# Two-block transformer stack on one core: feed-forward products of 512 columns on x and its rest side by side

## What is computed

```
def swiglu(h, w_in, w_out):                      # w_in 1024 x 5632, w_out 2816 x 1024
    gate, up = jnp.split(h @ w_in, 2, axis=-1)
    return (jax.nn.silu(gate) * up) @ w_out
...
for l in range(DEPTH):                           # first block
    x = x + 0.5 * swiglu(rmsnorm(x, ffn1_norm[l]), ffn1_w_in[l], ffn1_w_out[l])
    x = x + hybrid_mixer(rmsnorm(x, mix_norm[l]), ...)
    x = x + 0.5 * swiglu(rmsnorm(x, ffn2_norm[l]), ffn2_w_in[l], ffn2_w_out[l])
...
hf = rms_norm(x, g_ffn)                          # second block, end of a layer
x = x + jnp.square(jax.nn.relu(hf @ w_up)) @ w_down
```

## Time and profile before

| what | value |
|---|---|
| median of three runs | 2402.16 us |
| profiled execution, its own time | 2402.9 us |
| its span, first to last instruction | 2401.1 us |
| mean granted TensorE clock | 0.994 |
| TensorE matmul busy | 2356.1 us, 98% |
| weight loads busy | 2219.9 us, 92% |
| VectorE busy | 1588.1 us, 66% |
| ScalarE busy | 1402.8 us, 58% |
| GpSimd busy | 145.8 us, 6% |
| read from HBM | 382.89 MB, 160 GB/s over the span |

### The profile page before, as it was taken

One profiled execution on the slowest core, in us unless ns is written; L12 is line 12 of the kernel. 1 busy time (PEld: TensorE's weight loads), 2 busy tenths in 40 slices (PEclk: granted clock), 3 DMA queues, 4 the chain that ended last, 5 costly groups with the idle time before them and its releaser, 6 DMA issues. The chain is left out here.

```text
span 2401.1 us, 40844 instructions
## 1 busy us (share of the span) xinstructions
PE 2356.1 (98%) x17169; PEld 2219.9 (92%) x17169; DVE 1588.1 (66%) x1951; ACT 1402.8 (58%) x1872; POOL 145.8 (6%) x119
## 2 busy tenths in 40 slices
PE   8999999999999999999999999999999999999998
PEld 7998999999999999899999999899999989999998
DVE  5666668856666656667865656659785554978554
ACT  5455778465555645678835645546854444685443
POOL 0000002200000000001300000000030000004000
PEclk9999999999999999999999999999999999999999
DMA  6554544235555555444424555644555554455653
GB/s 226 194 177 158 158 141 141 89 97 167 193 183 186 177 192 184 151 141 141 127 68 141 173 196 177 199 138 126 157 166 187 195 184 149 124 153 168 206 184 123
DMA packets 312453, 386.57 MB, mean 161 GB/s; under 512 B 10812, under 2 KB 287440, under 8 KB 312272
## 3 DMA queue, kind: packets, MB, share of 16 engines
q1 hardware_dynamic: 311952, 383.86, 49.3%
q10 hardware_dynamic: 320, 0.11, 0.0%
HBM read 382.89 MB, written 1.06 MB: 160 GB/s over the span
## 5 line engine op out<-in xcount | busy, mean ns | idle before, releaser
L313 PE MATMUL bank<-xhi,whi 128*128 128x256 f32 x3712 | 1063.6, 287 | 4.2 <-DVE wlo L302 4.2
L315 PE MATMUL bank<-xhi,wlo 128*128 128x256 f32 x3712 | 1051.2, 283 | 0.0
L314 PE MATMUL bank<-xlo,whi 128*128 128x256 f32 x3712 | 1051.1, 283 | 0.0
L292 DVE TENSOR_TENSOR wlo<-raw,whi 128x2048 fp32r<-128x2048 f32 x354 | 817.3, 2311 | 206.5 <-ACT whi L276 204.0
L276 ACT ACTIVATE whi<-raw 128x2048 fp32r<-128x2048 f32 x355 | 676.4, 1906 | 203.6 <-PE bank L315 203.5
L313 PEld LDWEIGHTS bank<-xhi,whi 128*128 128x128 f32 x3712 | 713.1, 192 | 9.6 <-DVE wlo L302 4.5
L314 PEld LDWEIGHTS bank<-xlo,whi 128*128 128x128 f32 x3712 | 713.0, 192 | 4.8 <-issue 1.9
L315 PEld LDWEIGHTS bank<-xhi,wlo 128*128 128x128 f32 x3712 | 712.6, 192 | 0.0
L313 PE MATMUL bank<-whi,yhi 128*128 128x512 f32 x608 | 237.9, 391 | 0.0
L314 PE MATMUL bank<-wlo,yhi 128*128 128x512 f32 x608 | 237.4, 391 | 0.0
L315 PE MATMUL bank<-whi,ylo 128*128 128x512 f32 x608 | 236.6, 389 | 0.0
(11 more groups left out here) (404 smaller groups left out, 2958.1 us busy)
## 6 DMA issues: line engine op xcount, KB each, us to landing
raw<-in_w_in SPq DMA_DIRECT2D x92, 1024.0 KB, 5.2
raw<-in_ffn_w_in SPq DMA_DIRECT2D x88, 1024.0 KB, 5.1
raw<-in_ffn_w_out SPq DMA_DIRECT2D x44, 1024.0 KB, 4.9
raw<-in_w_gate SPq DMA_DIRECT2D x32, 1024.0 KB, 5.6
raw<-in_w_up SPq DMA_DIRECT2D x32, 1024.0 KB, 5.4
raw<-in_w_down SPq DMA_DIRECT2D x32, 1024.0 KB, 4.9
raw<-in_w_branch_b SPq DMA_DIRECT2D x8, 1024.0 KB, 5.3
raw<-in_w_branch_a SPq DMA_DIRECT2D x8, 1024.0 KB, 5.3
```

The source lines that it names most:

```text
L292: e.tensor_tensor(wlo[s][:], raw[s][:], whi[s][:].bitcast(F32), ALU.subtract).then_inc(lo_done[s], 1)
L313: e.matmul(o, ahi, bhi, start=start, stop=False, skip_group_check=True)
L314: e.matmul(o, ahi, blo, start=False, stop=False, skip_group_check=True)
L315: return e.matmul(o, alo, bhi, start=False, stop=stop, skip_group_check=True)
```

## The change

**Wide products.** `xhi` and `xlo` become the two halves of one tile `xx`, chunk by chunk, so that both lie side by side. For gate, up and the squared-ReLU's up, one matmul of 512 columns multiplies `whi` with both; a second, of 256 columns, adds `wlo` by `xhi` to the left half. The right half holds `whi` by `xlo`. A product now takes two banks; gate has banks 4 and 5, up has 6 and 7 in every block, and squared-ReLU products take the pairs in turns. ScalarE copies the two right halves to `low`, VectorE adds them to the left halves (`wide_low`, `wide_sum`), and what read the bank reads the sum.

```
-        xhi = sb("xhi", [P, KC, T], F32R)
-        xlo = sb("xlo", [P, KC, T], F32R)
+        xx = sb("xx", [P, KC, 2, T], F32R)
+        xhi, xlo = xx[:, :, 0, :], xx[:, :, 1, :]
...
+        def wide_part(e, n, banks, b, chunks, j=None):
+            s, _ = n
+            for c in chunks:
+                if j is not None:
+                    chunk_ready(e, j, c)
+                e.matmul(banks[b][:], as_in(whi[s])[:, c, b * P:(b + 1) * P], xx[:, c, :, :].rearrange("p i t -> p (i t)"),
+                         start=c == 0, stop=False, skip_group_check=True)
+                mm = e.matmul(banks[b][:, 0:T], as_in(wlo[s])[:, c, b * P:(b + 1) * P], xhi[:, c, :],
+                              start=False, stop=c == KC - 1, skip_group_check=True)
+            return mm
...
+        def wide_sum(e, o, banks):
+            for b in range(2):
+                up = e.tensor_tensor(o[:, b * T:(b + 1) * T], banks[b][:, 0:T], low[:, b * T:(b + 1) * T], ALU.add)
+            return up
+
+        def wide_low(e, banks):
+            for b in range(2):
+                up = e.activation(low[:, b * T:(b + 1) * T], banks[b][:, T:2 * T], ACT.Copy)
+            return up
...
+        gate_banks, up_banks = bank[4:6], bank[6:8]
...
             def gate_up(i):
-                if i >= 2:
-                    e.wait_ge(h_done, f * FF1_BLOCKS + i - 1)
+                before = f * FF1_BLOCKS + i - 1
                 if i:
-                    feature_product(e, gate_unit(r0, u0, i), gate_of(i), xhi, xlo)
+                    e.wait_ge(gate_dve, before * GATE_STEPS + SUMMED)
+                    wide_product(e, gate_unit(r0, u0, i), gate_banks)
+                    e.wait_ge(gate_dve, before * GATE_STEPS + UP_SUMMED)
...
-                feature_product(e, up_of(r0, u0, i), up_bank(i), xhi, xlo)
+                wide_product(e, up_of(r0, u0, i), up_banks)
...
             def scale_gate(i):
...
+                e.wait_ge(gate_act, n * ACT_STEPS + LOW_KEPT)
+                wide_sum(e, gbuf, gate_banks).then_inc(gate_dve, 1)
...
-                e.tensor_tensor(two(gbuf), two(gate_of(i)[:]), spread_two(), ALU.mult).then_inc(gate_dve, 1)
+                e.wait_ge(gate_dve, n * GATE_STEPS + SUMMED)
+                e.tensor_tensor(two(gbuf), two(gbuf), spread_two(), ALU.mult).then_inc(gate_dve, 1)
...
                 e.tensor_tensor(hbuf, eg, gbuf2, ALU.mult).then_inc(gated, 1)
+                e.wait_ge(multiplied[s], r + 1)
+                e.wait_ge(gate_act, n * ACT_STEPS + UP_LOW_KEPT)
+                wide_sum(e, ubuf, up_banks).then_inc(gate_dve, 1)
                 e.wait_ge(gated, 1 + n + 1)
-                e.wait_ge(multiplied[s], r + 1)
-                e.tensor_tensor(hbuf, hbuf, up_bank(i)[:], ALU.mult).then_inc(h_done, 1)
+                e.wait_ge(gate_dve, n * GATE_STEPS + UP_SUMMED)
+                e.tensor_tensor(hbuf, hbuf, ubuf, ALU.mult).then_inc(h_done, 1)
```

```
+                        if n == N1 - 1 and tap < 3:
+                            keep_last_dve(e, l, 2 - tap)
...
-                    e.wait_ge(*V["p_min"](l, 0))
-                    kk_pe(e, 0)
-                    pair_branch_pe(e, l, r0, u0, 0)
+                    def last_keys():
+                        e.wait_ge(*V["p_min"](l, 0))
+                        kk_pe(e, 0)
+
+                    pair_branch_pe(e, l, r0, u0, 0, last_keys)
...
             pair_scaled_dve(e, l, r0, u0, 0)
-            split_lo(e, unit(r0, u0 + N1 + 4))
             pair_min_dve(e, l, 1)
-            for b in (0, 1):
+            for b in (0, 2):
...
-            pair_scaled_dve(e, l, r0, u0, 1)
```

```
         @block.sync
         def _(e):
+            gain_load(e, "ffn1_norm", x_in)
             e.dma_start(x[:], d["x"].rearrange("b (t p) d -> p (b t) d", p=P)).then_inc(x_in, 16)
...
-            gain_loads(e, list(COL))
             e.dma_start(positions, d["positions_2"].to_broadcast([32, T])).then_inc(positions_in, 16)
```

More of the change, by code:

```diff
@@ L327, in feature_product, with wide_product, late_first_product @@
                                   c == 0, c == KC - 1)
+                if b == 0 and between is not None:
+                    between()
             mm.then_inc(multiplied[s], 1)
-        def late_first_product(e, n, o, j, first=False):
+        def wide_part(e, n, banks, b, chunks, j=None):
             s, _ = n
[L334 to L341, removed]
+            for c in chunks:
[6 more added lines that the diff above has]
+            return mm
+        def wide_product(e, n, banks):
+            s, _ = n
+            split_ready(e, n)
+            wide_part(e, n, banks, 0, range(KC))
+            wide_part(e, n, banks, 1, range(KC)).then_inc(multiplied[s], 1)
+        def wide_sum(e, o, banks):
[6 more added lines that the diff above has]
+            return up
+        def late_first_product(e, n, banks, j, first=False):
+            s, _ = n
             if first:
@@ L622, in ffn1_sync @@
                 load_unit(e, unit(r0, u0 + 3 * i - 1), cols_of(i, 0), as_in)
+                if l == 0 and u0 == 0 and i == 1:
+                    for name in list(COL)[1:]:
+                        gain_load(e, name, gains_in)
                 load_unit(e, unit(r0, u0 + 3 * i), cols_of(i, FF1), as_in)
@@ L1001, in pair_branch_pe @@
                 e.wait_ge(*V["oa_lo"](l, GROUPS - 1))
-            feature_product(e, unit(r0, u0 + N1 + 2 * n + 1), branch_out_bank(n), yhi, ylo)
+            feature_product(e, unit(r0, u0 + N1 + 2 * n + 1), branch_out_bank(n), yhi, ylo, between=between)
         def gate_bank(n):
@@ L1599, in mix1_delta_act @@
             pair_gate_act(e, l, r0, u0, 1)
-            for b in (2, 3):
+            for b in (1, 3):
                 e.wait_ge(*V["scattered"](l, b))
@@ L1722, in mix1_delta_dve @@
                 if s < LEVELS - 1:
-                    split_lo(e, unit(r0, u0 + N1 + 1 + s))
+                    split_lo(e, unit(r0, u0 + N1 + s))
             for g in range(GROUPS):
@@ L1736, in mix1_delta_dve @@
                                 b4(4 + g)[:, 0:2, :], ALU.subtract).then_inc(V["v_new"].sem, 1)
+            split_lo(e, unit(r0, u0 + N1 + 6))
             for g in range(GROUPS):
```

118 lines of the change are left out of this document (67 added, 51 removed).

## The result

The change did not pay: 2406.24 us (median of 13 runs, 2404.08 to 2411.65) against 2401.37 us of the kernel before (13 runs, 2395.96 to 2405.14), a ratio of 1.0027 with a 95% interval of 1.0018 to 1.0037, that is 6.6 us slower (4.3 to 8.9). The forecast was 2394.0 with a range of 2384 to 2408: the number lies inside the range only because the range reaches past the kernel before; it is 12 us from the centre and on the other side of no change, slower by more than its interval where faster was forecast. By the 0.3% used in the prediction it is no change, to which 0.36 was given, and 0.50 to faster.

What follows compares the result with a forecast made beforehand. TensorE was taken as the bound, a matmul in flight for 2356.1 of 2401.1 us. Gated passes +2.6, squared-ReLU -3.5, delta -7.0, setup -0.35 made -8.2 us; from the median 2402.16 that gave 2394.0, range 2384 to 2408.

Steps and rivals of the forecast that it cites:

- The products: Gate, up and squared-ReLU up: one 512 and one 256 matmul take 347 ns where three 256s took 360.
- the 1632 chunks of the prediction: Count of pairs, 16 x (72 + 30), by which each ns of pair distance is worth 1.6 us.
- Rival 2: Wide matmuls: cost beyond the columns is no fixed price, pair 356.4 ns, 3.6 saved, 2409 us; chance 0.16.
- New work on the other engines: Steady gated blocks: ScalarE's copies and VectorE's sums add 1.48 us ahead of the scale, costed at nothing.
- Rival 3: Gated blocks: `wlo` of the row unit comes 0.1 to 0.6 us late, each 0.1 costing 3.6 us; chance 0.18.
- the cover: Steady gated blocks: `wlo` of the row unit is ready 0.09 us before TensorE needs it, with nothing behind it.
- Block 0 and 1, last rows: Pass starts and ends: TensorE loses 2.03 us net by block 1, waits 2.37 at gated ends, 1.37 at squared-ReLU ends.
- Delta part and setup: Shorter waits for block copies and `keep_last` give 3.5 us a layer, 7.0; earlier x and constants give 0.35.
- the setup: Kernel start: the gains' load goes ahead of x, which with the constants comes later; -0.35 us.
- The two terms of the delta part: Per layer: block copies 2.3 us sooner; earlier query products after `keep_last`, 0.9 to 1.4 us; together 3.5.

Runs made afterwards that it cites:

- the fillers: Changed kernel with matmuls whose result nobody reads put into TensorE's new waits: block 1 and last rows 1.0011, 2404.14 us; block 1 alone, measured again, 1.0019, 2405.21 us.

## Why the prediction missed

**The products.** The step that failed first is "I take 347, so 13 ns saved a chunk". Measured: 353.0, 7.0 ns saved. At the 1632 chunks of the prediction that is 9.8 us. I had the turns' cost in the earlier trace rows, one 512 behind a 256 at 0.24, and averaged it away with single crossings from form to form, in which 0.114 for the other seemed to give it back; in a run of turns it was 235.5 + 117.5. Rival 2's pair, 356.4, was nearer, 3.4 ns off on the other side where mine was 6, and its reason (the cost beyond the columns is no fixed price) is half true: a settled 512 costs 16 ns beyond its 213.3, a settled 256 12 ns, and the turns 5 more. The rule of the Trainium skill that is named beside it (TensorE: Matmul & The Clock Gate, section Back-to-back issue gap) gave 2.5 saved; the trace says 7.0, and 11.7 with the forms grouped.

**New work on the other engines.** Right. In gated pass 1 the gate ends at 745.97 and the scale starts at 747.72, 1.75 later (0.21 before), so the new work is 1.54 where 1.48 was forecast:

```profile
746.93 0.76 DVE L355 TENSOR_TENSOR arena<-bank,arena 128x256 f32<-128x256 f32 x2 [4.22 <-ACT arena L360]
747.72 0.69 DVE L822 TENSOR_TENSOR arena<-arena 128x512 f32<-128x512 f32 x1
...
749.06 2.28 DVE L296 TENSOR_TENSOR wlo<-raw,whi 128x2048 fp32r<-128x2048 f32 x1
```

`wlo` is done at 751.34, the row unit starts at 751.62 and none of the steady blocks has a wait. Rival 3 falls. The slower pair lent the cover some 0.1 us, but even with the quicker grouped pairs it held.

**Block 0 and 1, last rows.** Right in mechanism and size. With the pair as measured, 2.03 and four units' gain of 0.115 make 2.49: the trace has 2.49 to 2.59. Last rows 2.26 against 2.37, in the first pass 1.63; squared-ReLU 1.15 against 1.37. Together some 1.5 us better than forecast.

**Delta part and setup.** -8.6 us (-5.5 to -11.5) against -7.35: right in the sum, with the setup at 0.8 to 0.9 rather than 0.35. The two terms of the delta part were each off, and that they add up is luck: the wait for the block copies fell by 1.6 us a layer where 2.3 was forecast (1.8 are left, not under 1.5), that for `keep_last` by 1.75 where at most 1.4 was. And the prediction's first reading, that only the delta part has recurring waits of over 2 us, missed one, which the change doesn't touch:

```profile
PE bank L2086 <- DVE arena L2318: 6.2, 4, 2.1
```

**What had no term.** The clock behind the waits, 5.8 us in the profiled execution, 4.3 to 6.0 by the fillers. And the row units of the gated passes, 5.50 for 5.47 in 32 steady blocks, 1.3 us with the rounding of the marks; no run asked why.

The sum made anew: -8.2 + 9.8 (pair) + 1.3 (row units) - 1.5 (waits) - 1.2 (delta, setup) = +0.2 without the clock, and 4 to 6 with it, against 6.6 (4.3 to 8.9). Two steps make the miss: 347 for a pair, and the clock, which the sum put at nothing. The pair is one that the rows of before could bound only from both sides; the clock is one that they showed, at 450.75, and that I passed over.

## What to carry to other kernels

A wait of TensorE of some 2 us can cost more than its length: read the clock, or the distances of the matmuls, in the 5 us behind it, before and after a change, and put a price on it; in this kernel filling such waits with useless matmuls was faster than leaving them empty. When matmuls of two widths replace three of one, group them by width within an accumulation; the turns took 4.7 of the 11.7 ns that widening saves a pair. And look at the block behind a norm, where added work meets engines that are late already: an order of its own for that one block was worth 10 us, nearly as much as the 11.4 us that the 1632 pairs save in turns.

## What was unexpected on the chip

- Alternating matmuls of 512 and 256 columns at full clock start 235.5 and 117.5 ns apart, in runs of eight 229.5 and 118.8. The second adding to the other half of the bank changes nothing (235.4 and 117.5).
- The slow stretch begins between 0.5 us before TensorE goes on and 1.5 us after it, so mostly or wholly while TensorE is fully busy again; in dense products the distances are nearly doubled for up to 3.4 us (43.65 to 47.03), which costs 1.1 to 1.6 us.
- The same program had 3, 3 and 0 of its four waits in block 1 followed by one, in three executions; the program with grouped forms 0 and 0. What decides it is open.
